# Output products of two attention layers, moved by halves into the last units of attentions B and D

## The reference, cut to what matters

```python
def even_layer(x, ...):
    h = rmsnorm_2(x, norm)
    qa, ka, va, qb, kb, vb, gate = _split(h @ w_in, SPLIT_E)
    oa = neighbourhood_attention(qa, ka, va, rpb)            # attention A, 8 heads of 64
    ob = attend_blocks(qb, kb, vb, D_HEAD ** -0.5)           # attention B, 8 heads of 64
    o = jnp.concatenate([oa.reshape(B, S, -1), ob.reshape(B, S, -1)], -1) * jax.nn.silu(gate)
    return o @ w_out

def odd_layer(x, ...):
    ...
    oc = attend_blocks(qc, kc, v_c, ...)                     # attention C
    od = diff_attend_blocks(qd1, qd2, kd1, kd2, vd, lam, ...)  # attention D
    od = rmsnorm_2(od, g_sub_d) * (1.0 - lam_init)
    o = jnp.concatenate([oc.reshape(B, S, -1), od.reshape(B, S, -1)], -1) * jax.nn.silu(gate)
    return o @ w_out

x = x + even_layer(x, ...)
x = x + odd_layer(x, ...)
```

## Time and profile before

| | us |
|---|---|
| three runs | 4169.43, 4183.79, 4185.41 |
| median | 4183.79 |
| the profiled execution | 4181.56 |
| its span (first to last instruction) | 4179.8 |
| TensorE busy | 3827.0 (92%) |
| DVE, ACT, POOL busy | 1798.5, 1296.0, 899.1 |
| mean granted clock of TensorE | 0.959 |

### The profile page before, as it was taken

The page is one execution under the profiler, slowest core; times in us unless marked ns, Lnnn a source line. Parts: engine busy times, 40 slices in busy tenths (PEclk is TensorE's granted clock), DMA queues, the critical chain, the costliest instruction groups (busy, mean ns, idle before and its releaser), DMA issues.

```text
span 4179.8 us, 51613 instructions
## 1 busy us (share of the span) xinstructions
PE 3827.0 (92%) x21728; PEld 2999.2 (72%) x21728; DVE 1798.5 (43%) x2260; ACT 1296.0 (31%) x1520; POOL 899.1 (22%) x528
## 2 busy tenths in 40 slices
PE   6999999999999999999998988899797999988868
PEld 5778887777778778888886665666574666766657
DVE  5464444553715531101125445366542555454561
ACT  3243333332410110000013333255513565433340
POOL 4212222222323433333224111110030001011001
PEclk8999999999999999999999999999898999999889
DMA  3111111111144321111122110100121001000011
GB/s 129 36 46 46 51 51 42 41 46 54 56 139 144 111 71 45 51 46 49 50 83 89 49 44 26 31 21 11 41 77 29 12 14 39 17 23 23 18 46 61
DMA packets 276489, 215.06 MB, mean 51 GB/s; under 512 B 15984, under 2 KB 254736, under 8 KB 276272
## 3 DMA queue, kind: packets, MB, share of 16 engines
q1 hardware_dynamic: 256400, 146.01, 12.3%
q10 hardware_dynamic: 19872, 65.94, 4.3%
HBM read 170.11 MB, written 37.75 MB: 50 GB/s over the span
## 4 chain that ended last, share of the span: by engine, by line
PE 77%; DVE 12%; ACT 6%; issue 3%; ACTq 1%; DMA 0%; SPq 0%; DVEq 0%; POOL 0%; POOLq 0%
PE ps L325 36%; PE ps L342 15%; PE ps L373 7%; DVE AR L1938 2%; DVE AR L1946 2%; PE ps L1005 2%; DVE SM L2597 2%; PE ps L587 2%; PE ps L307 2%; PE ps L1016 1%; PE ps L418 1%; PE ps L284 1%; DVE SM L2531 1%; PE ps L996 1%; PE ps L1027 1%
## 5 line engine op out<-in xcount | busy, mean ns | idle before, releaser
L2701 POOL CAST WH<-WR 128x1024 fp32r<-128x1024 f32 (+2 forms) x254 | 270.7, 1066 | 3102.6 <-DMA WR<-in_w_in 847.3
L2703 POOL TENSOR_TENSOR WL<-WR,WH 128x1024 fp32r<-128x1024 f32 (+2 forms) x254 | 589.6, 2321 | 20.3
L325 PE MATMUL ps<-XH,WH 128*128 128x512 f32 (+2 forms) x2240 | 574.6, 399 | 14.2 <-DVE AR L2215 7.4
L325 PE MATMUL ps<-XH,WL 128*128 128x512 f32 (+2 forms) x2240 | 556.1, 390 | 0.0
L325 PE MATMUL ps<-XL,WH 128*128 128x512 f32 (+2 forms) x2240 | 553.3, 389 | 0.0
L325 PEld LDWEIGHTS ps<-XH,WH 128*128 128x128 f32 (+2 forms) x2240 | 418.0, 189 | 115.6 <-issue 8.2
L325 PEld LDWEIGHTS ps<-XH,WL 128*128 128x128 f32 (+2 forms) x2240 | 418.6, 187 | 93.5
L325 PEld LDWEIGHTS ps<-XL,WH 128*128 128x128 f32 (+2 forms) x2240 | 416.1, 186 | 91.8
L1938 DVE TENSOR_TENSOR AR<-AR 128x512 f32<-128x512 f32 (+2 forms) x345 | 392.1, 1137 | 88.4 <-ACT AR L1473 39.4
L342 PE MATMUL ps<-ARR,WH 128*128 128x512 f32 x1600 | 394.0, 391 | 15.9 <-ACT ARR L1557 8.1
L342 PEld LDWEIGHTS ps<-ARR,WH 128*128 128x128 f32 x1600 | 301.7, 189 | 82.3 <-issue 9.5
(11 more groups left out here) (243 smaller groups left out, 5046.7 us busy)
## 6 DMA issues: line engine op xcount, KB each, us to landing
WR<-in_w_in SPq DMA_DIRECT2D x78, 512.0 KB, 3.7
WR<-in_w_ffn_in SPq DMA_DIRECT2D x44, 512.0 KB, 3.8
spill<-H ACTq DMA_DIRECT2D x32, 512.0 KB, 2.7
gates<-AR ACTq DMA_DIRECT2D x32, 512.0 KB, 2.9
AR<-gates SPq DMA_DIRECT2D x32, 512.0 KB, 3.4
H<-spill ACTq DMA_DIRECT2D x32, 512.0 KB, 6.8
WR<-in_w_in_e SPq DMA_DIRECT2D x26, 512.0 KB, 3.9
WR<-in_w_in_o SPq DMA_DIRECT2D x23, 512.0 KB, 4.0
```

The source lines that it names most:

```text
L325: mm = pe.matmul(pt[0:m, h * 512:h * 512 + 512], wp[:, slot, k, 0:m], xp[:, k, h * 512:h * 512 + 512], start=i == 0, stop=i == 3 * KD - 1)
L2701: pool.tensor_copy(hi, full).then_inc(s_whi, 1)
L2703: pool.tensor_tensor(lo, full, hi, ALU.subtract).then_inc(s_wsplit, 1)
```

## The change

`heads_out` becomes a generator that writes products over four of the eight tiles of o (nk = 4, `k0` the first of them), one for each output tile. The first eight (tiles 0 to 3, of attention A or C) are the side of the last steps of B (steps 26 to 33) and D (steps 28 to 32, 34, 38 and one after the loop); the other eight follow the loop. To have the operands by then, prep_b(3) isn't padded and the highs and lows move ahead (B: steps 18 to 23 and 25; D: 24 to 29 and 31), with two of the eight reloads ahead of each of highs 0 to 3. DVE gets a second set of eight additions per layer (`half_in`); the scaling of H in the even layer moves into it.

```diff
+        def pause(steps):
+            for _ in range(steps):
+                yield
...
+            def heads_out(name, w, at, k0):
+                def ready(i, k):
+                    if i < 4:
+                        pe.wait_ge(s_ehi, at + k0 + k + 1)
+                    if i >= 8:
+                        pe.wait_ge(s_elo, at + k0 + k + 1)
+                for f in range(KD):
+                    split_gemm((name, f), cols(w, f * P, k0=k0, nk=4), 4, lambda k: XH[:, k0 + k, :],
+                               lambda k: R(k0 + k), ready if f == 0 else None)
+                    yield
...
-            weave(att_b(), chain(8, prep_b(1), prep_b(2), prep_b(3)))
...
-            heads_out("wout_e", woe, 0)
+            weave(att_b(), itertools.chain(chain(8, prep_b(1), prep_b(2), prep_b(3)), pause(2),
+                                           heads_out("wout_e_half", woe, 0, 0)))
+
+            weave(heads_out("wout_e", woe, 0, 4), ())
+            J["wout_e"] = J[("wout_e", 0)]
...
-            weave(att_d(), chain(8, *[prep_d(h) for h in range(1, 4)]))
-
-            heads_out("wout_o", woo, KD)
+            half = heads_out("wout_o_half", woo, KD, 0)
+            weave(att_d(), itertools.chain(chain(8, *[prep_d(h) for h in range(1, 4)]), pause(4), itertools.islice(half, 5),
+                                           pause(1), itertools.islice(half, 1), pause(3), half))
+            weave(heads_out("wout_o", woo, KD, 4), ())
+            J["wout_o"] = J[("wout_o", 0)]
...
-            def reload():
+            def reload(ks=range(KD)):
                 act.wait_ge(s_spilled, 16 * KD * reloads[0])
-                for k in range(KD):
+                for k in ks:
                     act.dma_start(H[:, k, :], a["spill"][k]).then_inc(h_in[k], 16)
-                reloads[0] += 1
+                reloads[0] += ks[-1] == KD - 1
...
             def high_e():
                 act.wait_ge(filled[bank(("gb", 3))], turn(("gb", 3)))
-                reload()
                 for k in range(7):
+                    if k < 4:
+                        reload((2 * k, 2 * k + 1))
+                    if k == 6:
+                        yield
                     high(k, ("O", BASE["B"] - 1) if k < 4 else ("O", BASE["B"] + 8 * (k - 4) + 7))
                     yield
 
-            weave(att_b(), itertools.chain(chain(8, prep_b(1), prep_b(2), prep_b(3)), high_e()))
+            weave(att_b(), itertools.chain(chain(8, prep_b(1), prep_b(2)), prep_b(3), high_e()))
...
                 act.wait_ge(filled[bank(("gd", 3))], turn(("gd", 3)))
-                reload()
-                yield
                 for k in range(7):
-                    if k >= 4:
+                    if k < 4:
+                        reload((2 * k, 2 * k + 1))
+                    else:
+                        if k == 6:
+                            yield
                         act.wait_ge(s_od_done, k - 3)
...
-                    if name == "wout_e":
-                        STT(H[:, k, :], H[:, k, :], par("nf", k), A(24), ALU.mult, ALU.mult).then_inc(s_dve_step, 1)
-                        v.wait_ge(s_dve_step, tick(s_dve_step))
...
+            def half_in(name, at):
+                for k in range(KD):
+                    n = (name, k)
+                    v.wait_ge(h_in[k], at)
+                    if name == "wout_e_half":
+                        STT(H[:, k, :], H[:, k, :], par("nf", k), A(24), ALU.mult, ALU.mult).then_inc(s_dve_step, 1)
+                        v.wait_ge(s_dve_step, tick(s_dve_step))
+                    v.wait_ge(filled[bank(n)], turn(n))
+                    TT(H[:, k, :], H[:, k, :], PS[bank(n)][:, :], ALU.add).then_inc(freed[bank(n)], 1)
+                    v.wait_ge(freed[bank(n)], turn(n))
+                    yield
+
+            half = half_in("wout_e_half", 48)
+            weave(att_b(), itertools.chain(chain(8, prep_b(1), prep_b(2)), prep_b(3), lows(range(6)), pause(1), lows([6]),
+                                           itertools.islice(half, 7)))
             low(7)
+            weave(half, ())
...
+            half = half_in("wout_o_half", 64)
+            weave(att_d(), itertools.chain(chain(8, *[prep_d(h) for h in range(1, 4)]), lows(range(4)),
+                                           together(lows((4, 5)), half), itertools.islice(half, 1),
+                                           together(lows([6]), half), itertools.islice(half, 1),
+                                           pause(1), itertools.islice(half, 1), pause(3), itertools.islice(half, 1)))
             low(7)
+            weave(half, ())
```

More of the change, by code:

```diff
@@ L2654, in low, with lows @@
                 v.wait_ge(s_elo, tick(s_elo))
-            def lows():
-                for k in range(7):
+            def lows(ks):
+                for k in ks:
                     low(k)
                     yield
-            weave(att_b(), itertools.chain(chain(8, prep_b(1), prep_b(2), prep_b(3)), lows()))
+            def half_in(name, at):
[12 more added lines that the diff above has]
+                                           itertools.islice(half, 7)))
             low(7)
+            weave(half, ())
             residual_norm("wout_e", 4)
@@ L2676, in _, with together @@
             weave(att_c(), itertools.chain(chain(4, *[prep_c(h) for h in range(2, 8)]), chain(8, prep_d(0))))
-            weave(att_d(), itertools.chain(chain(8, *[prep_d(h) for h in range(1, 4)]), (None,), lows()))
+            def together(one, other):
+                for _ in zip(one, other):
+                    yield
+            half = half_in("wout_o_half", 64)
[3 more added lines that the diff above has]
+                                           pause(1), itertools.islice(half, 1), pause(3), itertools.islice(half, 1)))
             low(7)
+            weave(half, ())
             for k in range(KD):
```

## The result

| | us |
|---|---|
| before, median of 7 runs | 4183.79 (4169.43 to 4193.15) |
| changed, median of 7 runs | 4157.86 (4150.96 to 4166.82) |
| ratio, 95% interval | 0.9939 (0.9924 to 0.9953) |
| changed, the profiled execution and its span | 4150.96, 4149.0 |

The forecast of 4156 lies 2 us from the median, and the kernel is faster by 0.6%: 26 us, with the ratio's interval from 20 to 32. The profiled spans differ by more, 30.8 us, so the first thing to ask is where those are. The table of stretches of the changed kernel, with the columns of the earlier trace rows, is cut at the same events: the scores of B's unit 18, the end of the first halves, the end of the output product; then the scores of D's unit 24 and the same two ends. The last two rows are parts of the first and the third: B from step 27 on, D from its product 0 on.

The account below looks back on a forecast made before the run. TensorE bounds the output products, but idles 55.9 us in the last units of B and D. B gives 6.6 us and D 19.9, together 26.5 off 4181.6: 4155.1, stated as 4156, range 4141 to 4175.

Parts of the forecast that it names:

- The matrix work is only moved: Output products of both layers: eight moved halves are 43.5 us, and each output stage shortens by as much.
- half-clock start of product 0: First half product in D: TensorE starts it at half clock after a gap, 1.7 us more.
- 0.4 us a step for reload pairs: D, four steps from unit 24: a reload pair ahead of the high lengthens each 8.24 us step by 0.4.
- Each takes 6.42 + 5.44 = 11.86: B, steps 27 to 31: a plain step plus a half product, 11.86 us each, five of them 59.3.
- Four pairs at 0.79 us are 3.2 us: -2.9: B: reloads issued in pairs by ACT cost 3.2 us instead of one block's 6.09, saving 2.9.
- Those splits stay as bare as they were: B, up to unit 26's maximum: seven splits without products instead of two, five more at 2.42 us, +12.1 us.
- The covers: B's product steps: DVE's scaling (1.28 us) runs under the product, its sum (1.22 us) under the next scores; otherwise 1.2 a step.
- GpSimd's splits, taken at nothing: Sixteen weight splits inside attention: no cost assumed, though in D at most 3 x 1.66 = 5 us.
- Rival 1: Contention and late splits in D, nothing gained in B: 12.2 us gained, 4170 to 4172; chance 0.20.
- Rival 2: Larger gain from no half-clock start, free reloads and no 0.6 us waits in product steps: 40.7 us, 4143; chance 0.10.
- Rival 3: Half clock enters the products: one slow group each costs 28.5 us, two give 4213; chance 0.05.
- Rival 4: The change fills nothing, as TensorE was bound in those steps already: 4182 to 4184; chance 0.03.

Follow-up runs that it names:

- sp_reload: Kernel late with H's eight reloads issued by SP in place of ACT's four pairs, in both layers; 4146.63 us, ratio 0.9918.
- d_only: The change in attention D alone, B and its output product as in the kernel before; 4161.75 us against 4187.01, ratio 0.9943.
- late: Changed kernel with B's highs and lows 4 to 6 moved from bare steps 22, 23 and 25 beside products 0 to 2; 4151.29 us, ratio 0.9914.
- no_sum_b: Changed kernel without DVE's 16 sums of the first halves onto H and the eight scalings (output incomplete); 4155.36 us, ratio 0.993.
- no_split_b: Changed kernel without GpSimd's split of the weights of the 16 half products (output wrong); 4159.18 us, ratio 0.9934.

## Why the prediction was right, and where its terms were off

| from the stretch's start | forecast | measured |
|---|---|---|
| B: maximum of unit 26 | 74.8 | 75.5 |
| B: end of product 0 | 86.2 | 86.8 |
| B: product steps 27 to 31 | 59.3 | 61.9 |
| B: drain with products 6 and 7 | 16.6 | 16.7 |
| B: whole | 205.6 | 209.1 |
| D: product 0 starts | 39.9 | 40.2 |
| D: its end | 47.0 | 45.9 |
| D: end of step 31 | 81.5 | 81.6 |
| D: end of first halves | 113.0 | 113.1 |
| D: whole | 156.5 | 156.7 |

- "The matrix work is only moved": right. The second halves take 43.7 and 43.6 us, and splits, loads and smaller jobs keep pace: TensorE waits for none of them, only for ACT.
- D, 19.9 us forecast, 19.7 measured: right at each mark within 1.1 us, with two errors that cancel. The half-clock start of product 0 (1.7 us) did not come, its first four matmuls took 1.20 us. Steps 29 to 31 took 35.7 us for 34.5. The 0.4 us a step for reload pairs are what sp_reload took away (1.6). d_only shows that this gain is D's own.
- B, 6.6 us forecast, 3.1 by the two profiles and 1 against the undisturbed stretch. Two terms of the sum were mis-sized. "Each takes 6.42 + 5.44 = 11.86": four of them take 12.15 to 12.37, for a product between other jobs takes 5.67 us, not 5.44, and starts 6.56 us behind the scores; that is 1.5 us. The fifth takes 12.98, 1.1 us more than forecast, of which 0.9 are the operation held beside GpSimd's subtraction, a term that I had put at nothing. And "Four pairs at 0.79 us are 3.2 us: -2.9": a pair takes 0.81, but the block it replaces 3.78, so 0.5 was to be had. This hardly moved the forecast of B's length after the change (the maximum of unit 26 came 0.7 us late), since my starting point held the long issue; it made the gain 2.4 us too large. The bound that I set beside it, nothing saved, was near the truth; I took a single row of 6.09 us as the block's length, though the earlier trace rows showed the first two DMAs at 0.33 and 0.46.
- "Those splits stay as bare as they were", +12.1 us: the mechanism is right (late takes 7.1 us back for three of them), but I read the 2.42 us of a split as its price. It was the order within a step: DVE's low stood directly behind ACT's high. This the profile before showed, 2.25 us of DVE's idle ahead of each low, put down to ACT.
- The covers held for DVE's sums and scalings (no_sum_b). GpSimd's splits, taken at nothing, cost about 1 us in each layer (no_split_b).
- Rival 1 (contention in D) was there with 1 of its 5 us (no_split_b). Rival 2 had the full-clock start of D in it, and nothing else. Rival 3 (the half clock enters the products) is refuted by the granted clock of 1.00 over B's steps from 27 on and D's from product 0 on. The Trainium skill (TensorE: Matmul & The Clock Gate, "A second HAM failure mode: psum-queue depth-cycling") reports a kernel whose short idles between groups of matmuls made the clock fall again and again; these steps, with waits of 0.15 to 1.6 us, don't show it. Rival 4 is refuted by D. (For rival 3 I wrote that the end of B has gaps of up to 3 us; one, at the reloads, is 8.47.)
- That the median came within 2 us is partly luck. The two stretches gave 22.8 us of the 26.5 forecast (some 21 against the undisturbed B), and B's error of 4 to 6 us lies inside the scatter of the runs; the medians differ by 26, and the rest isn't located.

## What to carry to other kernels

Before idle time is filled with work moved from elsewhere, ask why it is idle: here a one-step shift between two engines' queues removed 16 us, where filling the same steps by hand brought 1. When both must be done, put the dependent small operations beside the moved work, not ahead of it. And take a price from a block of equal instructions only after a look at each: one of eight had 2.64 us of the 6.09.

## What the runs showed that I had not expected

- One DMA issue on ACT took 2.64 us, where the other seven of its block took 0.33 to 0.58; in the three other profiles that have this block in B it took 3.77 to 3.78 us in all.
- An operation of DVE on 128x1 elements, 0.16 us by itself, takes up to 1.24 us when it starts during GpSimd's subtraction, and ends within 0.03 us of it: in step 31 of B in three further profiles at 1.05 to 1.13, and with 0.48 and 0.54 us in steps 30 and 31 of D. This operation stands between a maximum and its exponential, and TensorE waits behind both.
- Untouched parts scatter by more than the change in B is worth: B's first unit starts at 2698.0 to 2711.7 us over the profiles. Some of it is the half clock. TensorE's timeline ahead of B, of the kernel before in its first profile, and then of the same kernel profiled again:

```profile
2683.32 2.98 PE L807 MATMUL ps<-AR,CST 128*128 128x512 f32 x4 [2.32 <-ACT AR L1610]
2686.09 3.41 PE L827 MATMUL ps<-CST,AR 128*128 128x2 f32 x16
2689.36 3.76 PE L325 MATMUL ps<-XH,WH 128*128 128x512 f32 x8
2692.92 2.71 PE L325 MATMUL ps<-XH,WL 128*128 128x512 f32 x8
2695.46 2.00 PE L325 MATMUL ps<-XL,WH 128*128 128x512 f32 x8
```

```profile
2693.20 3.68 PE L807 MATMUL ps<-AR,CST 128*128 128x512 f32 x4 [2.32 <-ACT AR L1610]
2696.71 1.84 PE L827 MATMUL ps<-CST,AR 128*128 128x2 f32 x16
2698.42 2.09 PE L325 MATMUL ps<-XH,WH 128*128 128x512 f32 x8
```

  The same program, the same idle of 2.32 us, and eight matmuls of 1.98 us take 3.76 in the one and 2.09 in the other: the slow time lasts through four blocks (mean granted clock 0.58 over 12.1 us) or one (0.51 over 3.5 us, 1.00 behind it).
- Inside attention a half product costs 5.67 us, in a row 5.44.
